# A gather queue that also waits for the landing of an earlier first-table gather

## What is computed

```python
def peer_ffn(h, w_q, sub_keys, u, v):
    ...                                    # expert (b, s, 8, 16) and gates from product keys
    def per_block(inp):
        xb, eb, gb = inp
        act = jnp.einsum('bthkd,btd->bthk', u[eb], xb).astype(jnp.float32)
        w = (gb * jax.nn.gelu(act, approximate=False)).astype(v.dtype)
        return jnp.einsum('bthk,bthkd->btd', w, v[eb])
```

## Time and profile before

| | us |
|---|---|
| median of 3 runs | 3602.31 (3581.03 to 3608.64) |
| span of the profiled execution | 3609.5 |
| PE busy | 2951.6 |
| DVE busy | 2279.9 |
| POOL busy | 1827.0 |
| ACT busy | 1090.3 |

### The profile page before, as it was taken

How to read it: one execution, slowest core, us unless ns; L and a number is a source line. 1 busy time by engine, 2 the same in 40 slices (tenths; PEclk the granted TensorE clock), 3 DMA queues, 4 the chain that set the end, 5 groups by cost and what they waited for, 6 DMA issues and landing times.

```text
span 3609.5 us, 40438 instructions
## 1 busy us (share of the span) xinstructions
PE 2951.6 (82%) x14096; PEld 1978.7 (55%) x14096; DVE 2279.9 (63%) x4939; ACT 1090.3 (30%) x2864; POOL 1827.0 (51%) x1672
## 2 busy tenths in 40 slices
PE   9999989999995766666666426799999967999995
PEld 7878876666562332332332204567776645777771
DVE  3440047876067586877877778866666677666665
ACT  3320035553123224323324212223232312322322
POOL 3332212221026666666666666676656665665556
PEclk9999999999998777778877666699999866999997
DMA  4322254332359998999999999999999999999998
GB/s 148 117 88 94 93 210 146 96 108 92 156 231 368 338 376 321 354 371 361 365 361 357 400 339 355 358 386 409 409 409 409 395 347 333 393 409 409 409 409 348
DMA packets 312859, 1089.82 MB, mean 302 GB/s; under 512 B 33232, under 2 KB 56400, under 8 KB 309344
## 3 DMA queue, kind: packets, MB, share of 16 engines
q0 software_dynamic: 221184, 805.40, 58.3%
q1 hardware_dynamic: 91488, 282.04, 20.7%
HBM read 1051.59 MB, written 35.72 MB: 301 GB/s over the span
## 4 chain that ended last, share of the span: by engine, by line
PE 21%; DMA 12%; DVE 11%; POOL 10%; issue 9%; another core or an unknown queue 7%; ACT 3%; POOLq 0%; ACTq 0%; DVEq 0%
DMA arena<-in_v_dram,idx_v 10%; PE small L1924 5%; POOL arena L1773 5%; PE acc L1806 5%; PE wide L1941 4%; POOL arena L1757 3%; DVE arena L2341 3%; POOL far_rows L1757 2%; DVE far_rows L2341 2%; DVE arena L2613 1%; DMA far_rows<-in_u_dram,idx 1%; PE wide L1846 1%; DMA arena<-in_u_dram,idx 1%; PE wide L1831 1%
## 5 line engine op out<-in xcount | busy, mean ns | idle before, releaser
L1773 POOL DMA_INDIRECT arena<-in_v_dram,idx_v x752 | 793.8, 1056 | 697.7 <-PE acc L1806 377.3
L1806 PE MATMUL acc<-arena 128*32 128x512 f32 x3008 | 495.8, 778 | 425.9 <-DMA arena<-in_v_dram,idx_v 234.3
L1757 POOL DMA_INDIRECT arena<-in_u_dram,idx x480 | 491.6, 1024 | 343.2 <-DVE idx L2574 191.2
L1806 PEld LDWEIGHTS acc<-arena 128*32 128x32 f32 x3008 | 100.4, 128 | 691.4 <-issue 546.0
L1924 PE MATMUL small<-pwq 128*128 128x256 f32 x2048 | 468.1, 382 | 5.7 <-issue 4.3
L1924 PEld LDWEIGHTS small<-pwq 128*128 128x128 f32 x2048 | 387.4, 191 | 88.1 <-issue 32.5
L2341 DVE CUSTOM_DVE_ANT_0 arena<-arena,wide 128x1024 f32<-128x1024 f32 x294 | 354.9, 1215 | 64.4 <-DMA arena<-in_u_dram,idx 36.9
L2341 DVE CUSTOM_DVE_ANT_0 arena<-arena,h 128x1024 f32<-128x1024 f32 x186 | 226.6, 1224 | 206.4 <-DMA arena<-in_u_dram,idx 184.1
L1757 POOL DMA_INDIRECT far_rows<-in_u_dram,idx x288 | 298.2, 1035 | 90.8 <-issue 84.8
L2341 DVE CUSTOM_DVE_ANT_0 far_rows<-far_rows,wide 128x1024 f32<-128x1024 f32 x176 | 212.6, 1215 | 64.3 <-DMA far_rows<-in_u_dram,idx 38.4
L2101 ACT ACTIVATE arena<-comb,w_v 128x32 f32<-128x32 f32 x768 | 199.2, 311 | 169.6 <-remote 91.1
(11 more groups left out here) (376 smaller groups left out, 4975.1 us busy)
## 6 DMA issues: line engine op xcount, KB each, us to landing
pwq<-in_uT_dram SPq DMA_DIRECT2D x128, 512.0 KB
pwq<-in_v_dram SPq DMA_DIRECT2D x128, 512.0 KB
arena<-in_w_nat_dram SPq DMA_DIRECT2D x6, 2048.0 KB, 8.8
nat_dram<-stage SPq DMA_DIRECT2D x48, 256.0 KB, 2.1
arena<-in_v_dram,idx_v POOLq DMA_INDIRECT x752
scanT_dram<-stage SPq DMA_DIRECT2D x22, 512.0 KB, 2.9
arena<-in_w_tr_dram SPq DMA_DIRECT2D x18, 512.0 KB, 3.8
arena<-csT_dram SPq DMA_DIRECT2D x8, 1024.0 KB, 5.2
```

The lines of the kernel that those rows point to most:

```text
L1757: pool.indirect_dma_start(out=u_row(g), out_offset=None, in_=peer_u, in_offset=bass.IndirectOffsetOnAxis(ap=idx[:, t % KEPT, n:n + 1], axis=0)
L1773: pool.indirect_dma_start(out=v_row(g), out_offset=None, in_=peer_v, in_offset=bass.IndirectOffsetOnAxis(ap=idx_v[:, t % KEPT, n:n + 1], a ...
L1806: last = pe.matmul(acc[c * QUAD:(c + 1) * QUAD, half * 512:(half + 1) * 512], spread_row(at), v_row(at)[:, half * 512:(half + 1) * 512], s ...
```

## The change

Every U gather of slots 22 to 380 gets a second wait, for the landing of the U gather two slots back. Every V gather that is issued in slots 20 to 380 (V rows 0 to 360) gets one for the landing of the U gather one slot back. Nothing else is touched; the waits on `dot_done` and `v_used` stay.

```diff
@@ gather_u
                     if g >= U_RING:
                         pool.wait_ge(dot_done, g - U_RING + 1)
+                    if LAG + 2 <= g < DENSE_AT:
+                        pool.wait_ge(u_landed[(g - 2) % U_RING], 16 * ((g - 2) // U_RING + 1))
                     pool.indirect_dma_start(out=u_row(g), out_offset=None, in_=peer_u,
@@ gather_v
                     elif V_RING <= g < SLOTS - FINAL:
                         pool.wait_ge(v_used, (g - V_RING) // SIDE + 1)
+                    if g + LAG < DENSE_AT:
+                        before = g + LAG - 1
+                        pool.wait_ge(u_landed[before % U_RING], 16 * (before // U_RING + 1))
                     pool.indirect_dma_start(out=v_row(g), out_offset=None, in_=peer_v,
```

## The result

| | median us | lowest to highest |
|---|---|---|
| before | 3603.0 | 3581.0 to 3608.6 |
| changed | 3898.2 | 3885.5 to 3903.0 |

These are four runs of each kernel; the table of times before has three of the four. The ratio is 1.082 (95% interval 1.078 to 1.085): 295 us slower, twice the 146 us that the prediction added up. The direction and the place were right, the size was not.

A forecast was written before the change was run, and what follows sets the result against it. In slots 22 to 381 POOL, issuing gathers, was taken as nearly its own bound, 2.54 of 3.035 us a slot. Terms 108 + 35 + 15 − 12 = +146 us on 3602 gave about 3750 us, range 3668 to 3880.

The forecast's parts named there:

- the redundancy of the U waits: U gathers, slots 22 to 380: V in slot n−1 already waited for U(n−2), so the wait is always met; cost 0.
- the recurrence: POOL's gathers: if the V wait binds, U(n+1) = U(n−1) + W + 1.27, two slots per W + 1.27.
- W: Time from a U gather's start on POOL to the dot that waited for it alone; taken as 5.4 us.
- the first term: V waits on U landings: a slot takes 3.335 us against 3.035, over 359 slots +108 us.
- Met waits at no cost: POOL's added waits: where already met they cost 0; at 0.3 us each, 720 would be 216 us.
- Surviving stalls, +35: V gathers waiting for v_used: what remains of today's stalls, mostly the long waits on PE acc, +35 us.
- SP's transfers, +15: Transfers issued by SP beside the gathers make U landings late: between 0 and 36 us, taken as +15 us.
- The lead, −12: POOL's lead at slot 381 falls from eight rows to about two, so DVE and PE end less far behind: −12 us.
- The landing time falls with the queue: Rival: with two or three gathers in flight W falls under 4.8 us; 3602 us, within 1%; same, chance 0.07.
- the faster one built on it: Rival: shorter queues free V rows sooner; at W = 4.3, 90 us gained, 3512 us; chance 0.03.
- Full-flow latency and full stalls: Rival: W stays at 6.12 and long stalls add in full, +359, 3961 us; heavier than the main case, chance 0.10.
- The upper end of the range, W = 5.8: Main case's upper end, slots 22 to 380: 180 + 86 + 15 − 0 = +281 us, 3883 us.

The follow-up runs named there:

- v_only: The changed kernel with the U waits left out, V waits kept: 3904.4 us, ratio to before 1.077.
- v_even: The changed kernel without U waits and with V waits only where the V row is even, every second slot: 3885.3 us, ratio to before 1.072.
- v_first: The changed kernel without U waits, its V landing wait written ahead of the wait on v_used so the gather carries it: 3836.9 us, ratio to before 1.059.
- u_only: The changed kernel with the V waits left out, U waits kept: 3695.7 us, ratio to before 1.020.

## Why the prediction was wrong

**What was right.** The binding place (V gathers wait for U landings), the redundancy of the U waits (`v_only`), the recurrence that gives a slot (W + 1.27)/2 (`v_even`), the unchanged step of 1.27 us (POOL's gathers after: busy 0.96 and 0.97 us, steps of 0.3), and the dense part, which neither gives nor takes (1434.9 against 1436.2 us). The typical landing time was also right: W = 5.4 was read from the earlier trace rows, the six pieces of the chain have 5.44 us, and the median over the stretch, where the trace has the landings, is 5.4.

**The step that failed** is the sentence "A POOL that is woken pays the wake-up as DVE does here, so W holds it." Where DVE stands waiting, its dot starts 0.02 or 0.13 us after a landing in nearly all cases. POOL's V gather started 0.76 us after it: 0.26 us because a gather that is released takes that long to start, and 0.50 because its landing wait was a separate instruction. The W of the first term was therefore too small. The recurrence read backwards from the measured 3.858 us a slot gives W = 2 × 3.858 − 1.27 = 6.45 us. That alone would be true by construction, but the timeline gives W by itself: from each U(n−1) to the V gather of slot n, slots 22 to 380, the mean is 6.45 us (median 6.20), and from there to U(n+1) 1.265 us. So W was 1.05 us more than assumed, which is 1.05/2 × 359 = 188 us, and the term of 108 us measured 296. The other three terms, +38 together, measured about nothing beyond it: 188 too little and 38 too much is the 150 us by which the sum fell short. Of the 1.05 us, 0.76 are the usual pick-up (136 us), 0.04 the typical landing (7 us), and the remaining 0.25 (45 us) are the longer pick-ups (about 0.07) and late landings. The longest wait, 7.3 us, was for a U gather that took 10.7 us to land.

**Met waits at no cost.** The earlier trace rows were read rightly: a separate wait that is met passes while the gather ahead of it runs, and so does the taking up of the gather behind it. What I had not asked is what the same form costs when it is *not* met. No row of before showed it, since every late wait there was carried by its gather.

**The other terms.** Surviving stalls, +35: measured 3.6 us of waits on PE in all, so nearly 0. Four slots now take 15.4 us instead of 12.1. The 3.3 us more were expected to absorb a stall only up to that length, yet even stalls like those of 8.14 and 10.8 us are gone. Why is not shown; the prediction took a long stall as fixed in length, whatever the pace. SP's transfers, +15: whatever they cost lies in the 45 us above, together with every other late landing, and the runs don't separate them. The lead, −12: not returned, and its reading was wrong. U(381) started at 2173.32 and its dot at 2179.55 before, and at 2466.33 and 2472.41 after: 6.2 and 6.1 us. The second row was misread: its 0.31 us is the plain step, in which a dot happened to end, not a wait for dot 373. By DVE's timeline dot 373 had started at 2164.77 and dot 376 ran at 2173.09, so POOL was five rows ahead, and DVE, with its other work of those slots done, took them at 1.14 us each.

**The rivals.** "The landing time falls with the queue" did not come about (5.44 us, not under 4.8), and neither did the faster one built on it. The Trainium skill, "DMA: Bandwidth & Descriptors", section "Anatomy of one DMA — SWDGE (gpsimd) path", has 2.0 us plus bytes over 436 GB/s, an estimate of 3.2 us for 512 KB by that page. The 5.44 us here disagree. They begin at the gather's start on POOL, but even without the 0.94 us for which POOL is busy with it 4.5 us are left. "Full-flow latency and full stalls" gave a nearer time, 3961 us, for the wrong reasons, so its nearness is luck: W did reach 6.45, but mostly by the pick-up and not by the landing, and hardly a stall on `v_used` remained. The upper end of the range, W = 5.8, was bounded by rows of landings alone; a bound on the pick-up was missing. GB/s in the stretch fell to 283, not 315, in keeping with the longer slot.

## What to carry to other kernels

A wait on something that the same queue started one step ago turns throughput into latency: the time of a slot becomes (landing + pick-up + step) divided by the slots that the loop spans. Before adding such a wait, compare its distance with the landing time; here one slot further back made it free. And where a gather needs two waits, look in the trace which one it carries; in these kernels it was the first one written, and writing the wait that is met last first saved 67 us.

## What the runs showed of the hardware

A gather on POOL whose carried wait is released starts 0.26 us later (`v_first`, and the first V gathers of the changed kernel). If the late wait is a separate instruction ahead of it, it starts 0.76 us later, and in every seventh slot about 1.19 us later. The chain shows 0.52 us of this before the sequencer gets to the next wait, L1758, so the gather appears to be taken up only after the wait has passed; this reading of the 0.52 us is argued, not shown. A 512 KB gather in the thin flow of the changed kernel lands 5.1 to 5.7 us after its start on POOL on the chain shown, 5.4 in the median of the stretch. In `u_only`, where gathers follow more densely, the median is 5.7, and the two on the chain shown took 6.26 and 7.14.
